# Attention values with V stationary and the probabilities of four heads moving; outputs stay turned for the output projection

## The reference: what is computed

```python
    probs = jax.nn.softmax(jnp.concatenate([scores, sink], axis=-1), axis=-1)[..., :-1]
    out = jnp.einsum('bnkgqs,bnskd->bnqkgd', probs.astype(vv.dtype), vv)
    return out.reshape(B, S, SWA_HEADS * hd)
...
    mix = jnp.concatenate([o_gla, o_swa], axis=-1) @ w_out[l]
    x = x + gt_a * mix
```

## Time and profile before

| | |
|---|---|
| median of 3 executions | 658.32 us (657.18 to 662.32) |
| profiled execution: its own time | 653.8 us |
| profiled execution: span, first to last instruction | 651.9 us |
| TensorE busy | 519.0 us (80% of the span) |
| VectorE busy | 256.2 us (39%) |
| ScalarE busy | 132.3 us (20%) |
| granted TensorE clock, mean | 0.901 of 2.4 GHz |

### The profile page before, as it was taken

One profiled execution on the slowest core, in us unless ns is written; L12 is line 12 of the kernel. 1 busy time (PEld: TensorE's weight loads), 2 busy tenths in 40 slices (PEclk: granted clock), 3 DMA queues, 4 the chain that ended last, 5 costly groups with the idle time before them and its releaser, 6 DMA issues.

```text
span 651.9 us, 7484 instructions
## 1 busy us (share of the span) xinstructions
PE 519.0 (80%) x2654; PEld 309.2 (47%) x2654; DVE 256.2 (39%) x585; ACT 132.3 (20%) x323; POOL 88.2 (14%) x170
## 2 busy tenths in 40 slices
PE   0498999989898989999736998978887787886500
PEld 0453654456766656455534554445454444552300
DVE  4678775835251544465560212111111121111046
ACT  3402243324141512120301111111111010110011
POOL 4000000000000000000232222122222222212000
PEclk9999999999798898999756999798889898998665
DMA  8997959441000040152237999999999999996074
GB/s 294 382 356 241 344 193 374 142 182 77 0 2 1 1 193 1 64 217 107 103 157 280 363 415 416 416 417 418 415 419 416 418 418 415 417 385 276 11 265 154
DMA packets 51795, 165.60 MB, mean 254 GB/s; under 512 B 10366, under 2 KB 11407, under 8 KB 43323
## 3 DMA queue, kind: packets, MB, share of 16 engines
q1 hardware_dynamic: 41912, 155.31, 60.9%
q0 software_dynamic: 5312, 8.48, 3.6%
q10 hardware_dynamic: 4546, 1.50, 1.1%
HBM read 159.16 MB, written 15.01 MB: 267 GB/s over the span
## 4 chain that ended last, share of the span: by engine, by line
PE 57%; DMA 27%; DVE 5%; issue 3%; ACT 2%; SPq 2%; ACTq 1%; POOL 1%; POOLq 0%; DVEq 0%
DMA wide<-in_w_up 22%; PE ps L1335 17%; PE ps L1567 9%; PE ps L1506 8%; PE ps L1581 4%; PE ps L1440 2%; PE ps L1561 2%; DMA xres<-in_x 2%; PE ps L1413 1%; PE ps L1474 1%; PE ps L1377 1%; PE ps L1525 1%; ACTq L687 1%; SPq L438 1%; PE ps L1428 1%
## 5 line engine op out<-in xcount | busy, mean ns | idle before, releaser
L1335 PE MATMUL ps<-ring,hreg 128*128 128x512 f32 (+1 forms) x320 | 130.4, 562 | 2.1 <-DVE hreg L966 2.1
L1567 PE MATMUL ps<-ring,proj 128*64 128x256 f32 x400 | 107.0, 428 | 27.2 <-DMA ring<-in_w_up 25.7
L1568 PE MATMUL ps<-ring,proj 128*64 128x256 f32 x400 | 107.2, 429 | 0.0
L1335 PEld LDWEIGHTS ps<-ring,hreg 128*128 128x128 f32 x320 | 60.6, 193 | 63.0 <-issue 57.8
L1567 PEld LDWEIGHTS ps<-ring,proj 128*64 128x64 f32 x400 | 59.7, 154 | 60.4 <-issue 22.9
L1241 DVE TENSOR_TENSOR proj<-proj,ps 64x256 f32<-64x256 f32 x32 | 13.5, 423 | 167.9 <-ACT proj L856 167.9
L619 POOL DMA_INDIRECT y_rows<-proj,hreg x33 | 32.9, 996 | 203.2 <-DVE proj L1247 187.6
L1568 PEld LDWEIGHTS ps<-ring,proj 128*64 128x64 f32 x400 | 59.6, 154 | 0.0
L1506 PE MATMUL ps<-wide,ring 128*128 128x512 f32 x128 | 56.4, 594 | 0.0
L937 DVE SCALAR_TENSOR_TENSOR wide<-wide,csil 128x512 f32<-128x512 f32 x72 | 49.1, 746 | 4.3 <-DMA wide<-in_ada_w 4.3
L1581 PE MATMUL ps<-ring,proj 128*64 128x512 f32 x200 | 48.1, 600 | 0.4 <-ACT proj L886 0.4
(11 more groups left out here) (260 smaller groups left out, 629.4 us busy)
## 6 DMA issues: line engine op xcount, KB each, us to landing
ring<-in_w_gate SPq DMA_DIRECT2D x25, 1024.0 KB, 19.9
ring<-in_w_up SPq DMA_DIRECT2D x25, 1024.0 KB, 23.6
ring<-in_w_down SPq DMA_DIRECT2D x25, 1024.0 KB, 19.3
wide<-in_ada_w SPq DMA_DIRECT2D x24, 1024.0 KB, 8.9
ring<-in_w_in SPq DMA_DIRECT2D x4, 2048.0 KB, 9.8
wide<-in_w_gate SPq DMA_DIRECT2D x8, 1024.0 KB, 20.9
wide<-in_w_up SPq DMA_DIRECT2D x8, 1024.0 KB, 23.9
wide<-in_w_down SPq DMA_DIRECT2D x8, 1024.0 KB, 21.6
```

The source lines that it names most:

```text
L1335: mm = pe.matmul(ps[bank_of(st)][:, 0:CW[ch]], hT[:, k, b * P:(b + 1) * P], win_sb[ch][:, k, :], start=k == 0, stop=k == KD - 1)
L1567: pe.matmul(ps[bank][0:TILE, 0:F], hx[:, k, :], wg_sb[w][:, k, :], start=k == 0, stop=k == KD - 1)
L1568: mm = pe.matmul(ps[bank][TILE:P, 0:F], hx[:, k, :], wu_sb[w][:, k, :], start=k == 0, stop=k == KD - 1)
```

## The change

Two reciprocal-weighted multiplies on VectorE scale `probs` in place, four heads at a time, ahead of the transposes; a new semaphore `probs_scaled` counts them, and the transposes wait for it in two halves. In `attn_value` V of one key-value head (64 columns) is the stationary operand and `probsT` of its four heads (4 x 128 = 512 columns) the moving one, written to partitions 0 to 63 or 64 to 127 of one PSUM bank: four matmuls, two in block 0. The result has head width on the partitions and tokens along the row, which is what `out_proj` needs as a stationary operand, so VectorE only copies it, and `mix_turn` transposes four tiles in place of eight. ScalarE's part of `mix_turn` is gone. `out_proj` takes the four attention tiles first and waits for `mix_copied` only ahead of the other four. Since the rows of the attention part now come in another order, `wout_sb` is loaded by three DMAs: one of 2 MB over 128 partitions and two of 1 MB over 64 partitions each.

```diff
             sp.wait_ge(turn_ready, TURN[("mod", NPC - 1)] + 1)
-            sp.dma_start(wout_sb, w_out_v).then_inc(wout_in, 16)
+            sp.dma_start(wout_sb[:, 0:4, :], w_out_v[:, 0:4, :]).then_inc(wout_in, 16)
+            for kv in range(SKV):
+                sp.dma_start(wout_sb[kv * HD:(kv + 1) * HD, 4:8, :],
+                             w_out[0, GH * DV + kv * 4 * HD:GH * DV + (kv + 1) * 4 * HD, :]
+                             .rearrange("(j d) n -> d j n", d=HD)).then_inc(wout_in, 16)
...
-                elif kind == "mix_turn":
-                    b = st[1]
-                    act.wait_ge(mix_turned, 2 * b + 2)
-                    act.activation(mixT[b % 2][:, 4:8, :], ps[4][:, :].rearrange("p (k t) -> p k t", k=4), ACT.Copy)\
-                        .then_inc(mix_copied, 1)
...
                     dve.wait_ge(probs_ready, (SH + 1) * (n + 1))
+                    lo = 0 if n else P
                     link(dve.tensor_tensor(sm[:, 4, :], sm[:, 2, :], sm[:, 3, :], ALU.add))
-                    dve.reciprocal(sm[:, 5, :], sm[:, 4, :]).then_inc(sums_ready, 1)
+                    link(dve.reciprocal(sm[:, 5, :], sm[:, 4, :]))
+                    for i in range(2):
+                        hs = slice(4 * i, 4 * i + 4)
+                        dve.tensor_tensor(probs[:, hs, lo:], probs[:, hs, lo:],
+                                          sm[:, 5, hs].unsqueeze(2).broadcast_to([P, 4, 2 * P - lo]), ALU.mult)\
+                            .then_inc(probs_scaled, 1)
...
                     dve.wait_ge(values_ready, n + 1)
-                    dve.wait_ge(sums_ready, n + 1)
-                    dve.tensor_tensor(proj[:, n, CSQ:CSK].rearrange("p (h d) -> p h d", h=SH),
-                                      ps[3][:, :].rearrange("p (h d) -> p h d", h=SH),
-                                      sm[:, 5, :].unsqueeze(2).broadcast_to([P, SH, HD]), ALU.mult)\
-                                          .then_inc(attn_out, 1)
+                    dve.tensor_copy(proj[:, n, CSQ:CSK], ps[3][:, :]).then_inc(attn_out, 1)
...
                 elif kind == "probs_turn":
                     n = st[1]
-                    pe.wait_ge(probs_ready, (SH + 1) * (n + 1))
                     if n >= 1:
                         pe.wait_ge(attn_out, n)
                     for h in range(SH):
+                        if h % 4 == 0:
+                            pe.wait_ge(probs_scaled, 2 * n + h // 4 + 1)
...
-                    for h in range(SH):
-                        kv = h // 4
-                        for cc in range(0 if n else 1, 2):
-                            mm = pe.matmul(ps[3][:, h * HD:(h + 1) * HD], probsT[:, h, cc, :],
+                    for cc in range(0 if n else 1, 2):
+                        for kv in range(SKV):
+                            mm = pe.matmul(ps[3][kv * HD:(kv + 1) * HD, :],
                                            proj[:, n - 1 + cc, CSV + kv * HD:CSV + (kv + 1) * HD],
+                                           probsT[:, 4 * kv:4 * kv + 4, cc, :],
                                            start=cc == (0 if n else 1), stop=cc == 1)
...
-                    for i in range(2):
-                        for k in range(4 * i, 4 * i + 4):
-                            lo = (CV if i == 0 else CSQ) + (k % 4) * P
-                            mm = pe.transpose(ps[3 + i][:, (k % 4) * P:(k % 4 + 1) * P], proj[:, b, lo:lo + P],
-                                              ident[:, :])
-                        mm.then_inc(mix_turned, 1)
+                    for k in range(4):
+                        mm = pe.transpose(ps[3][:, k * P:(k + 1) * P], proj[:, b, CV + k * P:CV + (k + 1) * P],
+                                          ident[:, :])
+                    mm.then_inc(mix_turned, 1)
...
-                    pe.wait_ge(mix_copied, 2 * b + 2)
-                    for k in range(KD):
-                        mm = pe.matmul(ps[5 + i][:, :], mixT[b % 2][:, k, :], wout_sb[:, k, 512 * i:512 * (i + 1)],
-                                       start=k == 0, stop=k == KD - 1)
+                    for k in [4, 5, 6, 7, 0, 1, 2, 3]:
+                        if k == 0:
+                            pe.wait_ge(mix_copied, b + 1)
+                        w = mixT[b % 2][:, k, :] if k < 4 else proj[:, b, CSQ + (k - 4) * P:CSQ + (k - 3) * P]
+                        mm = pe.matmul(ps[5 + i][:, :], w, wout_sb[:, k, 512 * i:512 * (i + 1)],
+                                       start=k == 4, stop=k == 3)
```

More of the change, by code:

```diff
@@ L239, in layer_kernel @@
             sem(n) for n in ('attn_turned', 'attn_copied', 'scores_ready', 'scores_masked'))
-        rowmax_ready, probs_ready, sums_ready, probs_turned = (
-            sem(n) for n in ('rowmax_ready', 'probs_ready', 'sums_ready', 'probs_turned'))
+        rowmax_ready, probs_ready, probs_scaled, probs_turned = (
+            sem(n) for n in ('rowmax_ready', 'probs_ready', 'probs_scaled', 'probs_turned'))
         probs_copied, values_ready, attn_out = (
@@ L586, in _ @@
                 elif st == ("out_proj", 3, 0):
-                    pool.wait_ge(mix_copied, 2 * NB)
+                    pool.wait_ge(mix_copied, NB)
                     for i in range(2):
@@ L1124, in _ @@
                     b = st[1]
-                    dve.wait_ge(mix_turned, 2 * b + 1)
+                    dve.wait_ge(mix_turned, b + 1)
                     dve.tensor_copy(mixT[b % 2][:, 0:4, :], ps[3][:, :].rearrange("p (k t) -> p k t", k=4))\
@@ L1489, in _ @@
                     else:
-                        pe.wait_ge(mix_copied, 2 * b)
+                        pe.wait_ge(mix_copied, b)
                     pe.wait_ge(gate_scaled, b + 1)
-                    for i in range(2):
-                        for k in range(4 * i, 4 * i + 4):
-                            lo = (CV if i == 0 else CSQ) + (k % 4) * P
-                            mm = pe.transpose(ps[3 + i][:, (k % 4) * P:(k % 4 + 1) * P], proj[:, b, lo:lo + P],
-                                              ident[:, :])
-                        mm.then_inc(mix_turned, 1)
+                    for k in range(4):
+                        mm = pe.transpose(ps[3][:, k * P:(k + 1) * P], proj[:, b, CV + k * P:CV + (k + 1) * P],
+                                          ident[:, :])
+                    mm.then_inc(mix_turned, 1)
                 elif kind == "out_proj":
@@ L1500, in _ @@
                     if b == 0:
-                        pe.wait_ge(wout_in, 16)
+                        pe.wait_ge(wout_in, 3 * 16)
                     else:
                         pe.wait_ge(x1_done, 2 * b - 1 + i)
-                    pe.wait_ge(mix_copied, 2 * b + 2)
-                    for k in range(KD):
-                        mm = pe.matmul(ps[5 + i][:, :], mixT[b % 2][:, k, :], wout_sb[:, k, 512 * i:512 * (i + 1)],
-                                       start=k == 0, stop=k == KD - 1)
+                    for k in [4, 5, 6, 7, 0, 1, 2, 3]:
[4 more added lines that the diff above has]
+                                       start=k == 4, stop=k == 3)
                     mm.then_inc(out_proj_done, 1)
```

## The result

The changed kernel takes **639.5 us** (median of 4, 637.6 to 642.0), the kernel before 657.8 us (median of 4, 656.4 to 662.3); the ratio is 0.972, 95% interval 0.967 to 0.978. Forecast were 640.1 us and a gain of 18.2; measured is 18.2. By the interval the gain is known only to lie between 14 and 22 us, so that the two agree to the last digit is luck.

A forecast was written before the change was run, and what follows sets the result against it. The prediction took TensorE's chain of projections and short attention matmuls, from 120 to 315 us, as the bound. Values 8.7, clock 7.2 and transposes 2.3 gave 18.2 us off the median of 658.3: 640.1 us, range 631 to 652.

The forecast's parts named there:

- One for one: Whole program: every microsecond by which the mixer ends earlier, the program ends earlier too; the expert stage has no own start.
- Values, 8.7 us: Value matmuls on TensorE in four blocks: two output halves overlap, saving 1.0, 2.8, 3.25 and 1.65 us, sum 8.7.
- Clock, 7.2 us: Blocks 1 and 2: TensorE's clock no longer falls, so stages behind the values take block 0's 6.24 us; saves 7.2.
- Transposes, 2.3 us: `mix_turn` on TensorE: four of eight transposes go in each block, saving 0.97 us in the first and 1.3 in three more.
- The third fall: Clock fall in the 2.71 us pause for VectorE's gate scaling, ahead of the first mixing transposes; was to stay.
- Scaling, nothing: VectorE's two multiplies ahead of the transposes: hidden behind TensorE's work, 1.2 and 0.9 us to spare in block 1; cost nothing.
- `wout_sb`, nothing: Output weights by three loads instead of one: landing with 50 us to spare even at a quarter of the rate; cost nothing.
- The rivals without overlap: Value matmuls: the two halves do not overlap, so only 5.4 us are gained, 653 us; chance 0.08.
- with visible multiplies: VectorE's scaling: multiplies doubled to 2.44 us make TensorE wait, costing 5.4 us, 645.5 us; chance 0.06.
- The clock rival: Blocks 1 and 2: the clock falls all the same, the 7.2 us go, about 648 us; chance 0.25.
- the rival that is slower than before: Value matmuls: no overlap and the clock falls in every block, 11.9 us slower, 670.2 us; chance 0.04.

The follow-up runs named there:

- the 3.67 us groups: Value groups of the changed kernel with V of both key-value heads as one stationary operand of 128 columns, into two banks; 644.0 us.
- the late-load kernel: The kernel before, with the last two small loads on ScalarE's queue (the router's biases) issued behind `low_turn`; 654.5 us.
- the kernel with doubled scaling: The changed kernel with a second multiply (by ones) ahead of each of the two scalings on VectorE; 645.9 us.
- the forms without overlap: The changed kernel with both heads' values written to partitions 0 to 63 of two banks, 645.4 us, or with V as one 128-column stationary operand, 644.0 us.

## Why the prediction was right

**One for one.** Right, as far as can be told. The chain in the mixer shrank by 18.5 us, and from the end of the output projection to the end of the span are 337.4 us before and 337.6 after. Over all profiles this tail takes 336.2 to 337.4 us with the old value matmuls (four profiles) and 335.2 to 339.5 with the new or widened ones (ten), so a microsecond or two given back to the expert weights would not be seen, while a large part of the 18 would be.

**Values, 8.7 us.** Measured 8.3: 0.9, 2.7, 3.1 and 1.65. The new group takes 1.94 us behind the pause and 1.08 in block 0, 0.14 and 0.13 more than I took; block 3's 1.87, priced from the down projection, is exact. The strided moving operand costs nothing that these rows show. The drain between tilings costs nothing more that can be seen: block 3's price held the 0.15 us of an entry already, and the stages behind the values take 6.40 us in the chain with either form, so an exit costs nothing visible.

**Clock, 7.2 us.** Measured 7.2 (10.22 and 9.81 us in the chain became 6.40 and 6.41). The size was right, and the mechanism is borne out from two sides: filling the pause cures it without the new form, and with the new form it is all but gone without filling. But two of my reasons were weak. That the group ends before the clock would fall was wrong as a reason: the 3.67 us groups do not bring it down, and in the late-load kernel it fell 0.9 us after the start of a group of the old form. And block 0, which I took as the proof that the pause is harmless, had been lucky, as the same kernel shows. With matmuls of 512 columns and the full pause the clock fell once in 24 blocks, blocks 0 to 2 of eight profiles, the one fall being in the kernel with doubled scaling; 18 of these blocks have the change's own form, 6 the forms without overlap. The old form had 7 falls in 9. That both of the profiled pair's falls went is the likely outcome and not a certain one.

**Transposes, 2.3 us.** Measured 1.3 for the last three and 1.5 from the first to the projection (5.36 to 3.87 us); I had 1.0 for it, as if the whole stage stayed at the lower clock. The third fall stayed, as forecast, but in this profile the clock rose again some 0.8 us before the stage was over; in the kernel with one stationary operand it did not, and there the stage's 4.51 us make the saving 0.85. So the 0.5 us too much are luck.

**Scaling, nothing.** Right, shown alone and doubled. **`wout_sb`, nothing.** Right: the loads landed 8.2 us (2 MB) and 15.4 us (the halves) after their issue.

The sum came out at 18.3 in place of 18.2 because the values' shortfall of 0.4 met the transposes' 0.5. The rivals without overlap and with visible multiplies are refuted by the profile after, and the kernels that force them show what they would have cost: 4.5 to 6.4 us by their medians, 6.1 to 7.7 in the chain from block 0's `gla_operands` to the end of the output projection (158.2 us in the changed kernel). The clock rival was the serious one: in 1 of 24 blocks it happens. In the rival that is slower than before, the stretch of block 3 in the same ratio is 4.0 us and not 4.1; it changes nothing.

## What to carry to other kernels

Where one operand has few columns, make it the stationary one and stream the other; if the outputs then fall into different halves of the partitions, the matmuls overlap as well, and an output that stays turned may save the next stage its transposes. Ask of every pause on TensorE what runs behind it: a pause of 1.8 us followed by matmuls of 64 columns cost some 3.6 us behind the values in each block where the clock fell (7 of 9), and two matmuls of waste in the pause bought that back. Two profiled executions can differ by something that has nothing to do with the change (here 6.4 us), so compare stages, not spans.

## What the runs showed that I had not expected

- The overlap of two output halves does not need alternation: 1.94 us for four matmuls in either order, 3.62 in the same half (of two banks).
- A DMA issue can hold its engine up, here by 2.5 to 9.8 us. It was the eighth small load in a row; issued 15 to 19 us later it took 0.35. That it waits for the loads ahead of it on the queue is the likely reason, not a shown one.
- The loads over 64 partitions moved at about half rate. While the two halves of `wout_sb` came in, the windows of the changed kernel show the DMA engines as busy as ever, at 201 to 225 GB/s, where the load over 128 partitions had run at 406 to 430:

```profile
149.00:150.00 1.00, 1.00 (x7) 1.00 1.05 430
...
156.00:157.00 1.00, 1.00 (x3) 1.00 1.01 225
157.00:158.00 1.00, 1.00 (x4) 1.00 1.03 213
```
